# Modulation tiles in fours in front of every second projection tile, in place of pairs in front of each

## The reference

```python
mod = silu(cond) @ w_mod + b_mod                 # w_mod: 2048 x 12288, two rows: c_ctx and c
sh_m, sc_m, g_m, sh_f, sc_f, g_f = split(mod, 6)
h = rmsnorm(x, norm_g[0]) * (1 + sc_m) + sh_m
u = h @ w_in                                     # 2048 x 5120
# four mixers on column groups of u: A differential attention, B RG-LRU scans,
# C neighbourhood attention, D GQA with qk-norm and rotary
x = x + g_m * rmsnorm(mixers(u) @ w_out, norm_g[1])
h = rmsnorm(x, norm_g[2]) * (1 + sc_f) + sh_f
a, g = split(h @ w_ffn_in, 2)
x = x + g_f * rmsnorm((silu(g) * a) @ w_ffn_out, norm_g[3])
```

## Time and profile before

| | |
|---|---|
| median of 3 runs | 1865.83 us (1863.76 to 1867.02) |
| profiled execution | 1866.84 us, its span 1865.0 us |
| PE busy | 1779.4 us, 95% of the span |
| DVE, ACT, POOL busy | 878.2, 657.9, 124.4 us (47%, 35%, 7%) |
| mean granted TensorE clock | 0.986 |
| queue that carries the weights | 298.99 MB, 42.9% of 16 engines |
| step starts (first L779 of step s) | 0: 50.10, 2: 74.41, 3: 84.65, 4: 95.36, 16: 224.10, 19: 258.96, 22: 295.73, 30: 388.91, 36: 468.63, 37: 481.91 |

### The profile page before, as it was taken

The page is one execution under the profiler, slowest core; times in us unless marked ns, Lnnn a source line. Parts: engine busy times, 40 slices in busy tenths (PEclk is TensorE's granted clock), DMA queues, the critical chain, the costliest instruction groups (busy, mean ns, idle before and its releaser), DMA issues.

```text
span 1865.0 us, 22141 instructions
## 1 busy us (share of the span) xinstructions
PE 1779.4 (95%) x9307; PEld 1514.0 (81%) x9307; DVE 878.2 (47%) x1214; ACT 657.9 (35%) x933; POOL 124.4 (7%) x167
## 2 busy tenths in 40 slices
PE   3999999999999996999999999999999999999995
PEld 0667666677677875999999999999999888888884
DVE  5345468733555668433333333333333455555553
ACT  2322254433354434322222222222222344444431
POOL 1000125430300002000000000000000000000000
PEclk9999999999999998999999999999999999999998
DMA  9777777775755241333333333333333333333321
GB/s 374 285 290 307 304 275 271 284 271 230 239 191 226 91 158 45 136 116 132 132 116 136 118 131 133 116 136 119 130 135 114 113 128 121 136 115 133 128 76 68
DMA packets 46298, 315.20 MB, mean 169 GB/s; under 512 B 5388, under 2 KB 7816, under 8 KB 8888
## 3 DMA queue, kind: packets, MB, share of 16 engines
q1 hardware_dynamic: 43328, 298.99, 42.9%
q0 software_dynamic: 2544, 11.59, 1.8%
q10 hardware_dynamic: 328, 3.21, 0.5%
HBM read 308.40 MB, written 5.37 MB: 168 GB/s over the span
## 4 chain that ended last, share of the span: by engine, by line
PE 91%; DVE 5%; DMA 2%; issue 1%; ACT 1%; POOL 0%; DVEq 0%; SPq 0%; ACTq 0%
PE ps L995 39%; PE ps L779 8%; PE ps L781 7%; PE ps L780 7%; PE ps L727 6%; PE ps L728 6%; PE ps L729 6%; PE ps L706 4%; PE ps L890 1%; PE ps L913 1%; DMA raw<-in_weights 1%; DVE wlo L1056 1%; DMA ident<-in_ident_c 1%; PE ps L949 1%; PE ps L903 1%
## 5 line engine op out<-in xcount | busy, mean ns | idle before, releaser
L1056 DVE TENSOR_TENSOR wlo<-raw,whi 128x1024 fp32r<-128x1024 f32 x376 | 459.1, 1234 | 809.3 <-ACT whi L407 809.3
L407 ACT ACTIVATE whi<-raw 128x1024 fp32r<-128x1024 f32 x376 | 392.0, 1058 | 859.8 <-PE ps L995 505.4
L995 PE MATMUL ps<-h_hi,whi 128*128 128x384 f32 x1408 | 471.6, 335 | 0.0
L995 PE MATMUL ps<-h_hi,wlo 128*128 128x384 f32 x1408 | 470.5, 334 | 0.0
L995 PE MATMUL ps<-h_lo,whi 128*128 128x384 f32 x1408 | 470.5, 334 | 0.0
L779 PE MATMUL ps<-whi,h_hi 128*128 128x512 f32 x672 | 280.6, 418 | 10.6 <-DVE wlo L1056 10.4
L995 PEld LDWEIGHTS ps<-h_hi,whi 128*128 128x128 f32 x1408 | 264.6, 188 | 0.0
L995 PEld LDWEIGHTS ps<-h_lo,whi 128*128 128x128 f32 x1408 | 264.5, 188 | 0.0
L995 PEld LDWEIGHTS ps<-h_hi,wlo 128*128 128x128 f32 x1408 | 264.4, 188 | 0.0
L781 PE MATMUL ps<-wlo,h_hi 128*128 128x512 f32 x672 | 263.6, 392 | 0.0
L780 PE MATMUL ps<-whi,h_lo 128*128 128x512 f32 x672 | 263.0, 391 | 0.0
(11 more groups left out here) (224 smaller groups left out, 1076.9 us busy)
## 6 DMA issues: line engine op xcount, KB each, us to landing
raw<-in_weights SPq DMA_DIRECT2D x284, 1024.0 KB, 4.9
xT<-in_x_t ACTq DMA_DIRECT2D x1, 3072.0 KB, 13.1
out<-x_sb POOLq DMA_DIRECT2D x3, 1024.0 KB, 4.7
x_sb<-in_x_sample POOLq DMA_DIRECT2D x1, 2048.0 KB, 12.4
gw<-in_lru_gate_w SPq DMA_DIRECT2D x4, 256.0 KB, 2.8
out<-U POOLq DMA_DIRECT2D x4, 256.0 KB, 5.5
nabias<-rpb_pad POOLq DMA_DIRECT2D x16, 64.0 KB, 4.9
x_sb<-in_x_prompt POOLq DMA_DIRECT2D x1, 1024.0 KB, 7.8
```

The costliest lines, as they stand in the source:

```text
L407: nc.scalar.activation(whi[:, 2 * (g % RING) + b], raw[:, t % RAW, HK * b:HK * b + HK].rearrange("p k n -> p (k n)"), ACT.Copy).then_inc(w ...
L995: return nc.tensor.matmul(ps[bank][:, 0:T], w[:, k % KH * P:(k % KH + 1) * P], xs[:, k, :], start=first, stop=last)
L1056: V.tensor_tensor(wlo[:, 2 * (t % RAW) + b], raw[:, t % RAW, HK * b:HK * b + HK].rearrange("p k n -> p (k n)"), whi[:, 2 * (g % RING) + b] ...
```

## The change

One function gives another list. In steps 2 to 39 an even step has no modulation tiles in front of it and an odd step has all four of its block; steps 0, 1 and the output projection are as they were. The block that is complete at a step is the same as before, and the number of tiles too.

```diff
 def mod_tiles(s):
 
     if s < IN_STEPS:
-        m, first = 2 + s // 2, s % 2 * 2
-        return m, [] if s == 0 else [0, 1, 2, 3] if s == 1 else [first, first + 1]
+        return 2 + s // 2, [0, 1, 2, 3] if s % 2 else []
     if s - IN_STEPS in (2, 3, 4, 5):
```

## The result

| | before | after |
|---|---|---|
| median (5 runs each) | 1867.02 us (1863.76 to 1871.65) | 1879.38 us (1875.48 to 1879.46) |
| profiled execution, its span | 1866.84, 1865.0 us | 1879.38, 1877.6 us |
| mean granted clock | 0.986 | 0.982 |

The ratio is 1.0065, its 95% interval 1.005 to 1.008: slower by 12 us. The forecast was 1870.1 us with a range of 1862.5 to 1876.

A forecast was written before the change was run, and what follows sets the result against it. PE, holding 91% of the chain of waits, was taken as the bound. Terms -4.9 + 1.8 - 0.5 + 1.9 - 0.6 + 4.4 + 3.7 - 1.6 = +4.2 us gave a median of 1870.1 us, range 1862.5 to 1876.

The forecast's parts named there:

- The sign: Whole kernel: slower, given 0.48, against 0.40 for the same and 0.12 for faster.
- Entries and exits, -4.9: Modulation groups, steps 2 to 38: 19 vanish, saving about 0.35 us each, less at nine; -4.9 us, bounds -2.9 and -6.7.
- The landing: Odd step's tile, asked for behind four modulation tiles: lands 4.8 to 4.9 us after its request, no queue remaining.
- rival (3): Odd tile lands late behind the queue, 1.5 us at each of 16, 22, 30, 36, 38: 1877 us, chance 0.18.
- Step 16, +1.9: Gates of step 16: PE arrives 1.9 us earlier, the convolution does not; +1.9 us, bounds 0 and +4.4.
- Step 4, +1.8: Start of step 4: PE waits for `h_lo` behind the eviction, losing 2.45 us instead of 0.6; +1.8 us.
- step 8's -0.5: Step 8: its estimated loss of 0.5 us goes, as its tile lands earlier seen from PE; -0.5 us.
- Step 22, +4.4: Gates of step 22: wait 3.9 us instead of 0.3, `modc` wait of 0.9 gone, clock loss 1.75; +4.4 us.
- Steps 28 to 36: Attention at even steps, no slack: +1.85 us in step 30, 0.15 for 28, 32 and 34 together; no clock loss.
- Steps 36 to 38: Step 36 waits +1.7 us for mixed weights; POOL's mask shifts in step 37: -3.0 or 0, half taken, -1.6.
- rival (2): Whole kernel faster: only saved entries show, ACT's and DVE's chains shorten with PE; -4.9 us, 1861, chance 0.12.
- Rival (1): Not slower: POOL's collision in step 37 goes, step 38 keeps slack, step 22 keeps the clock; 1865.0 us, chance 0.20.

The follow-up runs named there:

- the new order: Convolution (16, 19, 22, 25), attention gap 0 (even 28 to 38) and `h_hi` copies (3, 7, 11) put ahead of the split: fours 1855.79 us, pairs 1864.30 us.
- fours: The changed kernel, four modulation tiles in front of odd steps and none in front of even ones, against the kernel before: 1879.38 us, ratio 1.0065.
- pairs: The kernel before, with two modulation tiles in front of each step: 1867.02 us; as control with the new order 1864.30 us, ratio 0.9991.
- the first experiment: Fours with ACT's `lru_in` and DVE's `lru_conv` of steps 16, 19, 22 and 25 moved ahead of the next tile's split: 1872.07 us, ratio 1.0024.

## Why the prediction was wrong

The sign was its likeliest one and most terms hold. The step that failed is "It lands 4.8 to 4.9 us after that, so no queue remains.": the tile that mattered landed after 7.9 us, and step 16 lost 7.4 us (5.2 of wait, 2.1 of clock) where +1.9 was counted. Beside it one term was left at nothing, the clock behind a wait of under 2 us: 1.8 us in step 30.

1. **Entries and exits, -4.9: held within its bounds.** Where no wait stands on either side, two steps are 0.34 us shorter (10 to 12, with 0.35 predicted). In the new order, with waits of the same size, fours and pairs differ by 5.7 us from step 1 to 40, and by 8.5 by the medians; what makes up the rest of that is open.
2. **The landing: failed.** The sum took the batch at 14.9 us and the next request at 12.6, so 2.3 us of queue remained by its own figures, and a tile needs 2.5 behind that: 4.8, as good as none. In front of step 16 the first request came at 208.2 (the gate weights), the batch was through 15.3 us later and the odd tile asked for at 12.4, so 2.9 us of queue: near the forecast. But the tile then needed 5.0 us more instead of 2.5. The step of 2.5 us came from one batch at the start; most tiles keep it, some don't. Up to step 28 most other batches take 14.8 to 16.5 us, and the odd tiles land after 4.9 to 7.1 us, those asked for in steps 8 to 14 after 6.2 to 6.4. The margin was nil, and rival (3) had said so, for 0.18. It named five steps at 1.5 us each; what came was one at 3.1 us of landing and, in step 36, one at 1.3.
3. **Step 16, +1.9: mis-sized.** It measured a wait of 5.2 us and 2.1 of clock. "PE has nothing to spare" was right; with the load in time (the odd tile one place earlier) the wait is 2.13, near the 1.9 that I had. The stretch's bound of +4.4 left out the clock.
4. **Step 4, +1.8: held**, 1.78, and it goes when `h_hi` is put ahead. The stretch 2 to 16, with step 8's -0.5 in it, fits to 0.1 us. Step 19's wait went too, as forecast.
5. **Step 22, +4.4: wait right in size and wrong in place, clock too small.** PE waits 3.54 us in front of the step, for `wlo` of its own tile, not in front of the gates. On DVE the split stood behind the decay of the block before (`lo` began at 298.16), and PE asks for both halves before its first matmul. That is read from the time line; no run moved the decay. Behind the wait the clock is at 0.50, and from 301.68 to 308.06 us fifteen projection matmuls start 0.425 us apart instead of 0.227. That is 3.0 us, where I had 1.75. With the waits that went (0.9 for `modc`, 0.3 at the gates) it makes 5.3 for +4.4.
6. **Steps 28 to 36: wait right, clock left out.** 1.95 us in step 30 for +1.85. But the clock fell behind it, 1.8 us, where the prediction had taken 1.7 us of idle time as harmless from one window; and `kT` was waited for 0.81 us in step 28, where 0.15 stood for three steps (with a bound of 2.5). The two make up the 2.6 us by which this stretch missed.
7. **Steps 36 to 38: right in sum by luck.** In step 36 PE waits 3.11 us for the mixed weights instead of 1.7: the tile, issued at 479.6, needed 6.1 us, though the batch in front of it was through at 479.5 and `nabias` was asked for only from 485.05 on. Why is open. The clock stayed up. In step 37 POOL's mask met the split, its first half, which is near the worse of the prediction's two ways:

```profile
500.10 4.58 POOL L1567 TENSOR_TENSOR nabias<-nabias,tables 128x2048 f32<-128x2048 f32 x1 [5.27 <-DMA nabias<-rpb_pad]
```

```profile
501.17 5.73 DVE L1055 TENSOR_TENSOR wlo<-raw,whi 128x1024 fp32r<-128x1024 f32 x2 [5.17 <-ACT whi L406]
```

The split took 5.73 us instead of 2.36, but PE was late enough to wait only 1.13 (before, 3.13 and the clock). The Trainium skill (SBUF — State Buffer, "SBUF: two separate sides") says that GpSimd and a DVE instruction with two SBUF inputs hold a shared port pair in turn; the trace agrees: POOL had 3.5 of its 4.58 us left when the split began, and 2.36 + 3.5 is 5.9.

Against the faster rival (2): the chains on ACT and DVE did not shorten with PE; they came in time only where they no longer stood behind the split. Rival (1), the clock kept at step 22, did not come; what it said of the collision did in part.

## What to carry to other kernels

Work that looks removable, because it only fills PE, may be the time in which a load lands and the next engine gets on; before it is moved, look at what stands behind the load's consumer on each in-order engine, and put what PE needs in this step ahead of what it needs in the next. With that order the fours were 10 us faster than the kernel before instead of 12 slower, and the order alone gave 1.5 of them. A queue whose margin comes out at nil is to be priced from the slowest landings of the trace, not from its first batch.

## What the runs showed of the hardware that was not expected

**Idle time alone does not say whether the clock falls.** At full clock behind it: 3.11 us idle at 490 and 1.78 in front of step 4 (fours), 2.23 at 236 (tile two places earlier). At the lower level behind it, for a part of the window: 1.95 us at 406 in the fours, 2.31 in front of 291.18 in the fours with all work ahead, and in the first experiment behind 1.76 us in front of 478.04, whose windows are below. The same wait of 1.90 us in the same place of step 30 was followed by the lower level in the first experiment (395.28) and not with the odd tile one place earlier (397.86): 18.5 and 16.9 us for steps 30 to 31.

```profile
475.00:478.00 3.00, 1.28 (x6) 0.74 (x4) 2.92 (x6) 1.04 (x2) 3.00 (x6) 1.00 0.76 246
478.00:481.00 3.00, 2.96 (x8) 1.57 (x9) 1.09 (x3) 0.28 (x1) 3.00 (x6) 0.58 0.54 111
```

What decides between them stays open. The price of a fall in the fours was 2.1 us at step 16, 3.0 at 22 and 1.8 at 30.

**A load behind a queue can need more than its share.** Loads of 1 MB land 2.5 us apart when queued, but in many batches one lands 3.7 to 4.1 us after the one in front of it (203.8 after 200.1). The one issued at 220.7 landed 5.0 us after the one in front of it (211.84 + 11.72 = 223.56), with no other load asked for behind it. The odd tiles issued at 274.3 and 349.5 show it too, with 4.4 and 4.9 us. Windows of the fours over that time:

```profile
220.00:223.00 3.00, 2.13 (x13) 1.56 (x13) 0.69 (x1) 0.00 (x0) 0.00 (x0) 1.00 0.99 407
223.00:226.00 3.00, 3.00 (x15) 2.48 (x14) 0.00 (x0) 0.00 (x0) 0.00 (x0) 1.00 0.75 281
226.00:229.00 3.00, 3.00 (x15) 2.49 (x14) 0.00 (x0) 0.40 (x1) 0.00 (x0) 1.00 0.14 55
```

In its last 2.6 us the DMA engines are 14% busy: a small rest of the tile is late, and the whole split waits for it. Why was not tried.
